# Six early feature blocks, the first two projection phases as one of two passes, and the other modulation columns in whole rows through three places

## The reference, cut to what matters

```python
mod = silu(c) @ w_ada + b_ada                  # w_ada: 2048 x 12288, c: 1 x 2048
sh1, sc1, gt1, sh2, sc2, gt2 = split(mod, 6)
h = rms_norm(x, g_mix) * (1 + sc1) + sh1       # x: 256 tokens x 2048
z = h @ w_in                                   # w_in: 2048 x 11344, cut into columns:
# q_sb k_sb v_sb (1024 each), q_ds k_ds v_ds (1024 each), q_ix (1024), k_ix 64, w_ix 16, gate_sb 2048, gate_ds 2048
o_sb = stick_breaking_attention(q_sb, k_sb, v_sb)                     # 8 heads
o_ds = indexer_sparse_attention(q_ds, k_ds, v_ds, q_ix, k_ix, w_ix)   # 8 heads, keeps the 64 best keys of each query
merged = sigmoid(gate_sb) * (o_sb @ w_o_sb) + sigmoid(gate_ds) * (o_ds @ w_o_dsa)
```

## Time and profile before

| | |
|---|---|
| median of 3 runs | 2686.55 us (2686.44 to 2687.0) |
| span of the profiled execution | 2684.8 us |
| PE, DVE, ACT, POOL busy | 98%, 67%, 48%, 9% |
| transfers, mean over the span | 218 GB/s |

### The profile page before, as it was taken

One profiled execution on the slowest core, in us unless ns is written; L12 is line 12 of the kernel. 1 busy time (PEld: TensorE's weight loads), 2 busy tenths in 40 slices (PEclk: granted clock), 3 DMA queues, 4 the chain that ended last, 5 costly groups with the idle time before them and its releaser, 6 DMA issues.

```text
span 2684.8 us, 34364 instructions
## 1 busy us (share of the span) xinstructions
PE 2629.5 (98%) x12051; PEld 2166.7 (81%) x12051; DVE 1794.2 (67%) x2061; ACT 1290.9 (48%) x1558; POOL 228.6 (9%) x164
## 2 busy tenths in 40 slices
PE   2999999999999999999999999999999999999999
PEld 1887887888888888888888887887888888888887
DVE  7977776878777666666666865677555555555554
ACT  2545554445455444444444564556554444444443
POOL 0000000100000000000000310130001111111110
PEclk9999999999999999999999999999999999999999
DMA  9978777677786666666666556643666666666663
GB/s 391 389 269 301 270 259 256 209 251 264 291 286 230 205 202 205 202 204 203 203 203 189 188 172 184 190 145 126 203 186 191 188 192 190 188 192 190 189 194 134
DMA packets 280529, 585.56 MB, mean 218 GB/s; under 512 B 21776, under 2 KB 24236, under 8 KB 279540
## 3 DMA queue, kind: packets, MB, share of 16 engines
q1 hardware_dynamic: 280084, 583.61, 67.0%
q10 hardware_dynamic: 352, 0.71, 0.1%
HBM read 582.07 MB, written 2.11 MB: 218 GB/s over the span
## 4 chain that ended last, share of the span: by engine, by line
PE 94%; DVE 3%; DMA 1%; issue 1%; ACT 0%; SPq 0%; DVEq 0%; ACTq 0%
PE lin L482 29%; PE lin L484 29%; PE lin L483 29%; DVE sb_acc L1681 1%; DMA sb_raw<-in_w_in_dram 1%; PE aux L785 1%; DMA sb_ada<-in_w_ada_dram 1%; PE aux L516 1%; PE aux L959 0%; PE aux L573 0%; PE aux L796 0%; DVE sb_wlo L1586 0%; PE aux L482 0%; PE aux L484 0%; PE aux L483 0%
## 5 line engine op out<-in xcount | busy, mean ns | idle before, releaser
L1586 DVE TENSOR_TENSOR sb_wlo<-sb_raw,sb_whi 128x1024 fp32r<-128x1024 f32 x896 | 1103.6, 1236 | 781.0 <-ACT sb_whi L1014 777.6
L1014 ACT ACTIVATE sb_whi<-sb_raw 128x1024 fp32r<-128x1024 f32 x896 | 948.0, 1060 | 1219.6 <-PE lin L484 1134.9
L482 PE MATMUL lin<-sb_whi,sb_act_hi 128*128 128x512 f32 x2636 | 1045.1, 396 | 1.8 <-DVE sb_wlo L1586 1.0
L484 PE MATMUL lin<-sb_whi,sb_act_lo 128*128 128x512 f32 x2636 | 1027.4, 390 | 0.0
L483 PE MATMUL lin<-sb_wlo,sb_act_hi 128*128 128x512 f32 x2636 | 1026.3, 389 | 0.0
L482 PEld LDWEIGHTS lin<-sb_whi,sb_act_hi 128*128 128x128 f32 x2636 | 495.2, 188 | 107.0 <-issue 8.7
L484 PEld LDWEIGHTS lin<-sb_whi,sb_act_lo 128*128 128x128 f32 x2636 | 494.7, 188 | 104.6
L483 PEld LDWEIGHTS lin<-sb_wlo,sb_act_hi 128*128 128x128 f32 x2636 | 495.5, 188 | 100.2 <-issue 2.2
L482 PE MATMUL lin<-sb_whi,sb_hid_hi 128*128 128x512 f32 x704 | 275.4, 391 | 0.0
L484 PE MATMUL lin<-sb_whi,sb_hid_lo 128*128 128x512 f32 x704 | 274.2, 389 | 0.0
L483 PE MATMUL lin<-sb_wlo,sb_hid_hi 128*128 128x512 f32 x704 | 273.9, 389 | 0.0
(11 more groups left out here) (360 smaller groups left out, 1804.8 us busy)
## 6 DMA issues: line engine op xcount, KB each, us to landing
sb_raw<-in_w_in_dram SPq DMA_DIRECT2D x176, 512.0 KB, 5.9
sb_raw<-in_ffn_w_gu_dram SPq DMA_DIRECT2D x176, 512.0 KB, 3.7
sb_ada_in<-in_w_ada_dram SPq DMA_DIRECT2D x128, 512.0 KB, 4.1
sb_raw<-in_gla_w_in_dram SPq DMA_DIRECT2D x96, 512.0 KB, 3.8
sb_raw<-in_w_gate_dram SPq DMA_DIRECT2D x88, 512.0 KB, 3.8
sb_raw<-in_w_up_dram SPq DMA_DIRECT2D x88, 512.0 KB, 4.4
sb_raw<-in_w_down_dram SPq DMA_DIRECT2D x88, 512.0 KB, 5.6
sb_raw<-in_ffn_w_down_dram SPq DMA_DIRECT2D x88, 512.0 KB, 3.6
```

The source lines that it names most:

```text
L482: pe.matmul(o, h, whi[:, w], start=first and q == 0, stop=False)
L484: m = pe.matmul(o, l, whi[:, w], start=False, stop=last and q == 1)
L1014: act.activation(whi[:, idx % RING * HALF:(idx % RING + 1) * HALF], raw[:, idx // 2 % RING, idx % 2 * HALF:(idx % 2 + 1) * HALF], ACT.Copy ...
L1586: dve.tensor_tensor(wlo[:, c], raw[:, idx // 2 % RING, idx % 2 * HALF:(idx % 2 + 1) * HALF], whi[:, c].bitcast(fp32), ALU.subtract).then_i ...
```

## The change

- `EARLY` is 6: the 16 early rows are 0.79 MB each, through six places; the norm of x stands after add 6. `last_add` keeps its two parts.
- A and B become one phase A of 112 halves with 14 groups. The first pass takes three pairs of all groups (42 halves), the second five pairs (70 halves). ACT copies eleven groups out after the first pass, and DVE adds the second pass to them (`a_sum`); three groups stay in PSUM.
- The other ten blocks come in 16 rows of 1.31 MB, three places: `late_piece(k)` behind half 4+2k in SP's queue, `late_add(k)` after the remainder of half 5+2k. `first_columns(2)` (20 sums of 16 columns instead of 12 of 32) stands after half 38 instead of 25.
- The stick-breaking heads come every seven halves from half 55. `ada_columns` and `ffn_scale` move into C1. The index product stands after half 46.
- Chunks: one per 1.65 slabs in slabs 23 to 54, two per slab in slabs 56 to 61, 1.45 per slab in slabs 62 to 105 (2, 1, 2, 1, 1, 2, 1, 2 in slabs 68 to 75). `hankels` stands after the fifth slab (68) of C1's second iteration instead of the first (64). The number of halves, groups and chunks is the same.

```diff
-EARLY = 10
+EARLY = 6
-SLOTS = 4
+SLOTS = 6
+LATE_SLOTS = 3
-    ("A", 1, 48, 9), ("B", 4, 16, 2), ("C1", 1, 32, 4), ("C2", 2, 16, 2), ("O", 2, 16, 4), ("U", 2, 16, 2),
+    ("A", 1, 112, 25), ("C1", 1, 32, 4), ("C2", 2, 16, 2), ("O", 2, 16, 4), ("U", 2, 16, 2),
...
-    _at = 14 + _n * 10 // 16 if _n < 16 else 24 + (_n - 16) * 6 // 7 if _n < 44 else 4 + _n if _n < 64 else 11 + _n if _n < 96 else 13 + _n if _n < 107 else 17 + _n
+    _at = 23 + _n * 33 // 20 if _n < 20 else 56 + (_n - 20) // 2 if _n < 32 else 62 + (_n - 32) * 44 // 64 if _n < 96 else 13 + _n if _n < 107 else 17 + _n
...
         def late_piece(kt):
-            sp.wait_ge(sem("ada0_sum"), EARLY_ROWS if kt < SLOTS else EARLY_ROWS + kt - SLOTS + 1)
+            if kt >= LATE_SLOTS:
+                sp.wait_ge(sem("ada0_sum"), EARLY_ROWS + kt - LATE_SLOTS + 1)
+            else:
+                if kt == 0:
+                    sp.wait_ge(sem("tt_T"), KT // 2)
+                sp.wait_ge(sem("ada0_sum"), KT - 5 + kt)
...
+            if RING <= i < RING + 2 * KT and i % 2 == 0:
+                late_piece((i - RING) // 2)
...
-                if after and s == 0:
+                if after and s == 4:
                     after()
...
-            if kt == 7:
+            if kt == 6:
                 norm_stats(0)
                 norm_rows(X)
...
         def a_sum(n):
-            g, banks = A_AGAIN[n], lin[(0, 0, 0, 1, 0, 1)[n]]
             drained(0, "A", A_ENDS[n])
             for tb, free in ((0, free0), (1, free1)):
...
+                dve.wait_ge(free, 2 + GROUPS - A_HELD + n)
+                z = projected(A_AGAIN[n], tb)
+                dve.tensor_tensor(z, lin[n % 2][tb][:], z, ALU.add).then_inc(free, 1)
...
+        for kt in range(KT):
+            hk.setdefault(RING + 1 + 2 * kt, []).append(lambda kt=kt: late_add(kt))
```

More of the change, by code:

```diff
@@ new lines, in sb_turn @@
+        def sb_turn(h):
+            if h:
+                pe.wait_ge(sem("sb_qk"), h)
+            else:
+                pe.wait_ge(sem("wix_made"), 1)
+            pe.wait_ge(free0, 2 + GROUPS - A_HELD + (2 if h < NH // 2 else 5))
+            pe.wait_ge(free1, 2 + GROUPS - A_HELD + (2 if h < NH // 2 else 5))
+            for w in range(2):
+                for tb in range(TB):
+                    m = pe.transpose(aux[0][:, w * S + tb * P:w * S + (tb + 1) * P], head_of(sbz, w, tb, h), ident)
+            m.then_inc(sem("head_T"), 1)
@@ new lines, in sb_scores, with sb_suffix @@
+        def sb_scores(h):
+            pe.wait_ge(sem("sb_qk"), h + 1)
+            pe.matmul(aux[1][:, 0:S], qk_sb[:, S:S + P], qk_sb[:, 0:S], start=True, stop=True)
+            pe.matmul(aux[1][:, S:S + P], qk_sb[:, S + P:2 * S], qk_sb[:, P:S], start=True, stop=True).then_inc(sem("head_z"), 1)
+        def sb_suffix(h):
+            pe.wait_ge(sem("sb_lk"), h + 1)
+            pe.matmul(aux[2][:, 0:S], later, lk[:, 0:S], start=True, stop=False)
+            pe.matmul(aux[2][:, P:S], ones, lk[:, S:S + P], start=False, stop=True)
+            pe.matmul(aux[2][:, S:S + P], later, lk[:, S:S + P], start=True, stop=True).then_inc(sem("sb_suf"), 1)
@@ new lines, in _ @@
+        for i, (g, p) in enumerate(A_HALVES):
+            again = i >= A_FIRST
+            n = (i - A_FIRST) // (KT // 2 - A_PAIRS) if again else i // A_PAIRS
+            held = n < A_HELD if again else n >= GROUPS - A_HELD
+            banks = first_banks[(GROUPS - A_HELD + n) % 3] if again and held else lin[n % 2] if again else first_banks[n % 3]
+            if p == (A_PAIRS if again else 0) and not (again and held):
+                pe.wait_ge(free0, 12 + n if again else n)
+                pe.wait_ge(free1, 12 + n if again else n)
+            if n == 0:
@@ L638, in sb_values @@
[L638 to L654, removed]
@@ new lines, in held_drain, with late_pair @@
+        def held_drain(n):
+            act.wait_ge(half_used, A_ENDS[n])
+            bank = (aux[2], lin[1][0], lin[0][0])[n]
+            act.activation(projected(A_AGAIN[n], 0), bank[:], ACT.Copy).then_inc(free0, 1)
+        def late_pair(g):
+            act.wait_ge(sem("gs_made"), 3)
+            first_pair(g)
+        hk = {A_PAIRS * (n + 1) + 3: [lambda n=n: first_drain(n)] for n in range(GROUPS - A_HELD)}
+        for n in range(A_HELD):
+            hk[A_ENDS[n] + 3] = [lambda n=n: held_drain(n)]
@@ new lines, in weights, with hold_out @@
+        def weights(h):
+            act.wait_ge(sem("sb_sm"), h + 1)
+            act.activation(lb[:], lb[:], ACT.Exp).then_inc(sem("sb_ex"), 1)
+        def hold_out(h):
+            act.wait_ge(sem("head_o"), h + 1)
+            act.activation(oT_sb[:, h, :], aux[3][:, 0:S], ACT.Copy).then_inc(sem("sb_out"), 1)
+        for h, at in enumerate(HEADS_AT):
+            for off, step in ((4, hold_qk), (6, softplus), (9, weights), (11, hold_out)):
+                hk.setdefault(at + off, []).append(lambda h=h, step=step: step(h))
@@ L1180, in hold_q @@
+        body(0, "A", A_ENDS[-1], hk, start=RING)
         def hold_q(p):
@@ new lines, in _ @@
+        hk = {A_ENDS[n] + 3: [lambda n=n: held_drain(n) if n < A_HELD else a_sum(n)] for n in range(GROUPS)}
+        for kt in range(KT):
+            hk.setdefault(RING + 1 + 2 * kt, []).append(lambda kt=kt: late_add(kt))
+        for g in range(A_PAIRS, KT // 2):
+            hk.setdefault(LATE_PAIRS + g - A_PAIRS, []).append(lambda g=g: late_low(g))
+        hk.setdefault(LATE_PAIRS + KT // 2 - A_PAIRS, []).append(split_ix)
+        hk.setdefault(A_ENDS[1] + 3, []).append(hold_wix)
+        SC = HD ** -0.5
@@ new lines, in weights @@
+        def weights(h):
+            dve.wait_ge(sem("sb_suf"), h + 1)
+            dve.tensor_tensor(lb[:], lb[:], aux[2][:, 0:3 * P], ALU.add).then_inc(sem("sb_sm"), 1)
+            dve.wait_ge(sem("sb_ex"), h + 1)
+            dve.tensor_tensor(lb[:], lb[:], sbmask, ALU.mult).then_inc(sem("sb_a"), 1)
+        for h, at in enumerate(HEADS_AT):
+            hk.setdefault(at + 6, []).append(lambda h=h: log_keep(h))
+            hk.setdefault(at + 9, []).append(lambda h=h: weights(h))
+        body(0, "A", A_ENDS[-1], hk, start=RING)
```

300 lines of the change are left out of this document (120 added, 180 removed).

## The result

The changed kernel takes 2709.46 us (median of 4 runs, 2706.85 to 2710.74) where the kernel before takes 2686.76 (2686.44 to 2687.0): a ratio of 1.0081, 95% interval 1.0067 to 1.0095. It is slower by 22.7 us. The forecast was 2688.0 with a range of 2676 to 2697; the time lies above the range.

What follows compares the result with a forecast made beforehand. PE was taken to bound the kernel (94% of the chain); start -16.0, column sums +1.7, heads -1.9 and +0.7, C1's tail +15.6, C2 and O +1.0 summed to +1.1, giving 2687.7, rounded to 2688 us, range 2676 to 2697.

## What to carry to other kernels

In a queue that is served in order, a transfer that waits for a consumer holds up all that stands behind it. Ask how far ahead of its consumer the queue stands when it is held, not how long it is held. Place such a transfer as late in the queue as its own landing allows: moved two slabs back, the same transfers with the same waits cost 17 us less, and then some adds already waited 5 to 9 us for their chunk. No run went later. And when work is moved out of an early phase, price the loop (wait, transfer, copy, consumer) in each later phase that takes it in, with that phase's own rows; if a chain there needs an engine to be ahead, any work put on that engine in front of it is paid one for one.

## What was not expected of the hardware

Behind the late column sums the granted clock fell to half (1.2 of 2.4 GHz) though PE had not been idle: 40 matmuls of 16 columns ran for 4.6 us, and the matmuls of 512 columns behind them were 0.43 us apart instead of 0.23. The 24 of 32 columns before the change (2.6 us) left it at full. Stretches of the changed kernel, clock third from the end:

```profile
159.50:162.00 2.50, 2.50 (x24) 2.46 (x23) 0.00 (x0) 0.00 (x0) 0.00 (x0) 1.00 0.60 220
162.00:164.00 2.00, 2.00 (x19) 2.00 (x18) 0.00 (x0) 0.00 (x0) 0.00 (x0) 0.93 0.03 8
164.00:166.00 2.00, 2.00 (x6) 1.63 (x6) 0.41 (x3) 1.13 (x3) 0.00 (x0) 0.50 0.18 16
168.00:170.00 2.00, 2.00 (x11) 1.65 (x10) 1.50 (x2) 1.97 (x4) 0.00 (x0) 1.00 1.04 402
```

And each of the two long waits was paid twice: 6.9 and 5.6 us of idle time were each followed by a stretch at 0.50. From the first sparse scores to `ds_probs(0)` PE took 11.2 us instead of 9.3, and U's first part lost 2.9.
